# Sixteen small transfers in the first weight chunk of each expert, and all six norms ahead of the last sums

## The reference, cut to what matters

```python
def expert_choice_ffn(h, w_router, w_gate, w_up, w_down):
    ...
    aff, idx = lax.top_k(probs.T, cap)
    xe = t[idx]
    hid = jax.nn.silu(jnp.einsum("ecd,edf->ecf", xe, w_gate)) * jnp.einsum("ecd,edf->ecf", xe, w_up)
    ye = jnp.einsum("ecf,efd->ecd", hid, w_down) * aff[..., None].astype(h.dtype)
    out = jnp.zeros_like(t).at[idx.reshape(-1)].add(ye.reshape(-1, d))
    ...
    x = x + expert_choice_ffn(rms_norm(x, norm_ffn_w), w_router, w_gate, w_up, w_down)
    ...
    return rms_norm(x, norm_final_w)
```

## Time and profile before

| what | value |
|---|---|
| median of 3 runs | 2408.66 us (2408.6 to 2409.93) |
| the profiled execution | 2407.7 us, of which the span below is 2405.8 us |
| mixer, from the span's start | to about 1,015 us |
| experts, 16 times about 85 us | to about 2,388 us |
| last norms, stores, indirect writes | to 2405.8 us |
| PE busy / DVE / ACT / POOL | 99% / 45% / 22% / 13% of the span |

### The profile page before, as it was taken

One profiled execution on the slowest core, in us unless ns is written; L12 is line 12 of the kernel. 1 busy time (PEld: TensorE's weight loads), 2 busy tenths in 40 slices (PEclk: granted clock), 3 DMA queues, 4 the chain that ended last, 5 costly groups with the idle time before them and its releaser, 6 DMA issues.

```text
span 2405.8 us, 49544 instructions
## 1 busy us (share of the span) xinstructions
PE 2370.5 (99%) x21931; PEld 1625.6 (68%) x21931; DVE 1077.1 (45%) x2059; ACT 519.3 (22%) x1076; POOL 302.5 (13%) x417
## 2 busy tenths in 40 slices
PE   9999999999999999999999999999999999999997
PEld 8888999899898888745655455555555555444454
DVE  7989888888987634451221222122122112212213
ACT  6445444544534412200000000000000000000001
POOL 0422431341341000000000000000000000000001
PEclk9999999999999999999999999999999999999998
DMA  5233234223336545799999999999999999999996
GB/s 187 74 110 123 92 99 134 90 92 118 114 117 212 208 140 207 289 395 410 418 411 420 416 409 420 408 417 409 418 417 408 419 416 409 420 406 416 420 409 259
DMA packets 88646, 707.02 MB, mean 294 GB/s; under 512 B 11824, under 2 KB 16048, under 8 KB 51568
## 3 DMA queue, kind: packets, MB, share of 16 engines
q1 hardware_dynamic: 65504, 628.96, 64.4%
q0 software_dynamic: 14368, 56.80, 7.5%
q10 hardware_dynamic: 8560, 18.10, 2.0%
HBM read 669.76 MB, written 34.06 MB: 293 GB/s over the span
## 4 chain that ended last, share of the span: by engine, by line
PE 47%; DMA 10%; DVE 0%; issue 0%; POOL 0%; POOLq 0%; SPq 0%; ACT 0%; DVEq 0%
PE p_gu L2653 31%; PE p_y L2671 8%; DMA raw<-in_w_e 7%; PE p_y L2674 4%; PE p_z L2674 2%; DMA raw_first<-in_w_e 2%; DMA raw<-xa 1%; PE p_gu L1592 1%; DVE raw L2587 0%; DMA out<-raw 0%; DVE xg L2579 0%; POOLq L2725 0%; POOL out L2489 0%; PE off_banks L1606 0%; SPq L2421 0%
## 5 line engine op out<-in xcount | busy, mean ns | idle before, releaser
L2653 PE MATMUL p_gu<-raw,xT 128*32 128x512 f32 (+1 forms) x8160 | 888.6, 556 | 2.3 <-DMA raw<-in_w_e 2.2
L2653 PEld LDWEIGHTS p_gu<-raw,xT 128*32 128x32 f32 x8160 | 393.8, 110 | 362.8 <-issue 231.0
L2538 DVE SCALAR_TENSOR_TENSOR tg<-tg,p_gu 128x256 f32<-128x256 f32 (+1 forms) x144 | 57.4, 399 | 1051.6 <-ACT tg L2501 1047.1
L2671 PE MATMUL p_y<-raw,hidT 128*32 128x384 f32 x3744 | 433.3, 486 | 0.0
L1282 PE MATMUL pp<-h,wx_hi 128*128 128x256 f32 (+1 forms) x1664 | 423.9, 346 | 0.5 <-ACT fo L836 0.5
L2501 ACT ACTIVATE tg<-p_gu 128x256 f32<-128x256 f32 (+1 forms) x144 | 52.8, 367 | 1266.6 <-PE p_gu L2653 1249.0
L2674 PE MATMUL p_y<-raw,hidT 128*32 128x256 f32 x1248 | 319.5, 379 | 0.0
L1282 PEld LDWEIGHTS pp<-h,wx_hi 128*128 128x128 f32 x1664 | 282.9, 190 | 31.0 <-ACT fo L836 0.7
L1282 PE MATMUL pp<-h,wx_lo 128*128 128x256 f32 (+1 forms) x832 | 281.3, 338 | 0.0
L2674 PEld LDWEIGHTS p_y<-raw,hidT 128*32 128x32 f32 x1248 | 137.2, 110 | 100.1 <-issue 32.1
L2674 PE MATMUL p_z<-raw,hidT 128*32 128x256 f32 x624 | 184.8, 379 | 0.0
(11 more groups left out here) (297 smaller groups left out, 2951.1 us busy)
## 6 DMA issues: line engine op xcount, KB each, us to landing
raw<-in_w_e SPq DMA_DIRECT2D x185, 2048.0 KB, 32.0
raw<-in_w_e SPq DMA_DIRECT2D x58, 1536.0 KB, 32.5
raw_first<-in_w_e SPq DMA_DIRECT2D x23, 2048.0 KB, 33.3
w_raw<-in_w_x SPq DMA_DIRECT2D x48, 512.0 KB, 3.5
dec<-acs POOLq DMA_DIRECT2D x48, 512.0 KB, 4.8
raw<-in_w_e SPq DMA_DIRECT2D x16, 1024.0 KB, 32.6
w_raw<-in_w_g SPq DMA_DIRECT2D x24, 512.0 KB, 3.4
g_tab<-gx POOLq DMA_DIRECT2D x8, 1152.0 KB, 6.0
```

The costliest lines, as they stand in the source:

```text
L2538: dve.scalar_tensor_tensor(out=tg[:, r % 2, 0:w], in0=tg[:, r % 2, 0:w], scalar=1.0, in1=p[:, 0:w], op0=ALU.add, op1=ALU.mult).then_inc(s_ ...
L2653: mm = pe.matmul(p_gu[g][quad(q), 0:w], xT[:, e % 2, k * SLOTS + 32 * g:k * SLOTS + 32 * (g + 1)], slot[:, at:at + w], start=(k == 0), sto ...
L2671: pe.matmul(y_first[half][quad(g), :], hidden(g), w[:, half * 3 * P:(half + 1) * 3 * P], start=first, stop=last)
```

## The change: a split load and a new order at the end

The first "gu" chunk of experts 1 to 15 (15 chunks) is no longer one transfer. Its first 3584 columns come in one transfer of 128 partitions; its last 512 columns come in 16 transfers of 8 partitions each, 2 KB in a partition, 16 KB in all. The eight partitions of a piece lie four apart in one quarter of 32. All 17 add to the same semaphore, and the waits of the slot count them (`landings`). At the end of the program DVE does all six norms before both sums, and the roots are made in portions of three, two and one tile.

```diff
+LOW_COLS = 512
+EIGHTS = [slice(32 * q + r, 32 * (q + 1), 4) for r in range(4) for q in range(4)]
+
+def in_pieces(c):
+    kind, b, i = chunk(c)
+    return c >= RAW and kind == "gu" and i == 0 and b % NB == 0
+
+def landings(c):
+    return sum(16 * (1 + len(EIGHTS)) if in_pieces(n) else 16 for n in range(c % RAW, c + 1, RAW))
...
-    sp.dma_start(raw[c % RAW][:, 0:w], src).then_inc(s_raw[c % RAW], 16)
+    own = w - (LOW_COLS if in_pieces(c) else 0)
+    sp.dma_start(raw[c % RAW][:, 0:own], src[:, 0:own]).then_inc(s_raw[c % RAW], 16)
+    if own < w:
+        for rows in EIGHTS:
+            sp.dma_start(raw[c % RAW][rows, own:w], src[rows, own:w]).then_inc(s_raw[c % RAW], 16)
...
-        SQUARES_AT = ROUNDS - 1
-        NORMS_AT = ROUNDS - 1
-        ROOTS = (slice(0, 1), slice(1, 3), slice(3, NT))
-        FIRST_NORMS = 3
+        SQUARES_AT = {ROUNDS - 1: range(NT)}
+        ROOTS = (slice(0, NT // 2), slice(NT // 2, NT - 1), slice(NT - 1, NT))
...
-                if r == NORMS_AT:
-                    for t in range(FIRST_NORMS):
-                        norm(t)
+            for t in range(NT):
+                norm(t)
             summed(0)
             summed(1)
-            for t in range(FIRST_NORMS, NT):
-                norm(t)
...
-                pe.wait_ge(s_raw[c % RAW], (XT_LOADED if c % RAW < EARLY_RAW else 0) + 16 * (c // RAW + 1))
+                pe.wait_ge(s_raw[c % RAW], (XT_LOADED if c % RAW < EARLY_RAW else 0) + landings(c))
```

More of the change, by code:

```diff
@@ L2522, in _ @@
                         result(e)
-                if r == SQUARES_AT:
-                    for t in range(NT):
-                        square(t)
+                for t in SQUARES_AT.get(r, ()):
+                    square(t)
             act.wait_ge(f_row, 1)
```

## The result

The change takes **2447.6 us** (2445.7 to 2448.5), the kernel before 2409.4 us beside it: a ratio of 1.0158, with a 95% interval of 1.0144 to 1.0172. A sixth execution, at a granted clock of 0.586, took 4147.7 us and is in none of these numbers. The change is 38 us slower, where 2 us less were forecast. The profiled execution took 2445.7 us, with a span of 2443.8.

A forecast was written before the change was run, and what follows sets the result against it. PE and DMA engines were taken as overlapping limits, with 4.8 us of PE waits. That gain, inside the end's -1.9 us, took the profiled 2407.7 to 2405.8; 1.0 for the median gave 2406.8 us, range 2403 to 2414.

The forecast's parts named there:

- The bound: Weight loads: transfers lose 1.35 us per expert on PE; 13.9 us of growth are free, then PE waits, 4.8 us.
- the price of an end: First chunk's pieces: 16 packets and 16 ends on each of eight engines, taken as 0.2 us per expert.
- The 12 ns: Weights' DMA queue: what a packet costs beyond its bytes, from averages over the whole span; 16 to 32 make 0.2 to 0.4 us.
- the eight are the early ones: First chunk's pieces: they land on the eight early engines, which lose 0.83 us per expert; the others gain 0.63; chance 0.73.
- the late half: DMA engines at the end: eight that finish weights about 21.5 us after the others, 1.4 us for each of 15 experts.
- the first rival: First chunk's pieces go to the late eight: growth 2.18 us per expert, PE waits 16.6 us, 2423.4 us; chance 0.09.
- the fetches: PE's instruction packets, 16 KB, seven per expert: hinted extra duty of the late engines, 0.85 us each if they are eight.
- SP's issues: SP's queue: 16 issues of 0.328 us, 5.2 us more per expert, priced at nothing because earlier loads keep engines busy.
- The second rival: DMA queue holds a number of transfers, not bytes; pieces run at issue pace, 5.2 us per expert: 2476 us; chance 0.06.
- The end: Norms, sums and last product: indirect write at S + 20.45; the new order alone costs 2.9 us with the old S.
- S: Start of the first square of a row tile at the program's end: 2381.13 before, forecast 2376.3.
- the signs named beforehand: Profile signs of wrong: longer plateau of 0.5, share gaps at each expert's first load, old growth, first square later than 2378.

The follow-up runs named there:

- the 124-row run: Kernel before, with the last 128 columns of each first chunk loaded as two transfers, of 124 rows and of four: 2411.0 us, 1.0005.

## Why the prediction was wrong

**The bound.** It was read rightly: growth per expert beyond 13.9 us is paid by PE. With the measured 3.77 us per expert, the prediction's own form gives 14 x 3.77 - 13.9 - 4.8 = 34.1 us, and with 2.9 for the end 2445.7 us against 2447.6 measured. The size of the growth was wrong, by two steps.

**First failed step: the price of an end.** "16 to 32 of these are 0.2 to 0.4 us; I take 0.2, since an end carries no data." The sixteen pieces cost the slowest engines 2.42 us per expert, not 0.83; the three runs with 128 columns, with twice the ends and with the pieces spread show that the price goes with the number of transfers in a row and hardly with bytes. With the 0.63 us that the shorter main load saves, the sixteen take (2.42 + 0.63)/16 = 0.19 us of an engine each; with 128 columns it is (89.13 - 85.17 - 1.35 + 0.16)/16 = 0.17, and 0.155 for each that was added. The 12 ns came from an average over packets of which few carry an end, and nearly all such ends follow eight large packets, under which they disappear. The end's own packet is as short as that in the change (9 ns); what was left out is that one engine's semaphore updates come 0.20 us apart. Of the 3.05 us that the pace gives for the sixteen, 1.9 us are seen in the packets right behind the main load; where the rest goes is open. Of the gap between 2406.8 and the result, the price of the ends is 14 x (2.42 - 0.83) = 22 us. The Trainium skill (DMA: Bandwidth & Descriptors, "Why a DMA increments its semaphore by 16 and not by 1") says that each engine's last descriptor is a write that lands only after that engine's data. The trace agrees on the order: the updates of the late engine above come after the last piece's data, from 2238.65 on. What such a write costs, only the runs show.

**Second failed step: "the eight are the early ones", or else the late ones.** Both halves were taken whole. The plateau of 2/16 shows a third case: two of the eight that take the pieces are slowest. The count of the engines that lead shows that just two of the eight belong to the late half. That the plateau's two are these is argued: both take pieces (at 2235.1 and 2236.8, where the others' runs of sixteen end by 2219.1), and no other engine that does has a second duty of that size. The 2.42 us above rests on it. The time is set by the slowest engine, so two overlapping engines cost as much as eight: the first rival's mechanism, which alone would have given 2423.4, 16.6 us more than the forecast. That rival's chance of 0.09 was an argument without a row. With the 22 us of the ends that is the 39 us up to 2445.7.

What stays open: whether the fetches are the second duty, since no run took them away; and what the one engine has that ends last with pieces of four or two rows. In the kernel before one of the early eight lags too, 8.4 us behind the first about 2281, where the other seven are within 3.6; that it is the same engine is not shown.

**SP's issues** were priced at 16 x 0.328 = 5.2 us and at nothing. They are 16 x 0.657 = 10.5 us, and nothing was right (SP held for 12 us: 1.0002). The second rival, a queue that holds a number of transfers, had its place in gaps of the DMA share, and there are none (1.03 and 0.99 behind the pieces). SP's long issues from 1329 on do speak for a full queue, but the pieces follow one another on an engine in 0.086 us, not at the 0.657 us of an issue, and the 137 us of such issues in the 124-row run cost nothing. So its warning against small transfers was right, its price not.

**The end** was right in size. Write 20.35 us behind the first square, against 20.45 forecast; the order alone cost 2.5 us, against 2.9. Two errors inside it cancel: POOL's three roots follow one another, so the last norm ended at 2429.76, S + 13.4 in place of S + 12.3; the last product began 1.9 us behind the sums, not 3.0. That the order "pays only if S falls below 2378.2" was not put to the test: S rose to 2416.3.

Of the signs named beforehand, the ones for "wrong" came: a first square later than 2378, and a plateau, though not at 0.5. A plateau's height is the number of late engines, and the prediction asked only for its length.

## What to carry to other kernels

Work that is dealt out to 16 engines ends with the slowest one. Before moving bytes between them, find which engines are slow and which a short transfer takes: the height of the DMA share's plateau at the end counts the late ones. A transfer has a price on each engine besides its bytes, here 0.15 to 0.20 us, which shows only when small transfers follow one another; put large ones between them, or make fewer.

## What the runs showed of the hardware

- An eight-row transfer takes SP 0.657 us to issue, where a 128-row load takes 0.328 us.
- On an engine, transfers in a row cost 0.15 to 0.19 us each, with 512-byte rows as with 2048-byte rows (89.13 and 88.94 us an expert); the semaphore updates of one engine come 0.20 us apart. Spread among large ones, sixteen cost 0.94 us in place of 2.42.
- Two transfers of eight adjacent rows per expert cost 222 us in all: 231 to 251 GB/s on all engines for 20 us. Sixteen of eight rows of 2 KB, four apart, cost 36 us in all.
- While the pieces pass, the DMA share stays at 1 and the rate falls to 328 GB/s: a share of 1 is not a full rate, since a held-up packet (2.08 us in place of 0.61) counts as busy.
- Eight of the 16 engines fall behind the others in the kernel before: 11.1 to 13.0 us about 1688, 20.9 to 23.6 us about 2281.
